# Interleaving the first two column parts at both phase changes of an encoder layer, with eight of the sixteen residual chunks turned through scratch memory

## What is computed

```
h = h + 1/2 * post1(SwiGLU_1(pre1(h)))          # 2048 -> 2*5632 -> 2048
u = pre2(h); q,k,v,gates = u @ w_in             # two kinds of attention, heads of 128
h = h + post2((sigmoid(gate_A)*A + sigmoid(gate_B)*B) @ w_out)
h = h + 1/2 * post3(SwiGLU_2(pre3(h)))
```

## Time and profile before

| | |
|---|---|
| time, median of 3 runs | 2030.08 us (2029.84 to 2030.23) |
| the profiled execution | 2030.19 us, span 2028.4 us |
| PE busy | 2019.1 us (100% of the span) |
| DVE, ACT busy | 1236.8 us (61%), 1043.1 us (51%) |
| granted TensorE clock | 0.999 |
| transfers | 445.94 MB, 220 GB/s over the span |

### The profile page before, as it was taken

How to read it: one execution, slowest core, us unless ns; L and a number is a source line. 1 busy time by engine, 2 the same in 40 slices (tenths; PEclk the granted TensorE clock), 3 DMA queues, 4 the chain that set the end, 5 groups by cost and what they waited for, 6 DMA issues and landing times.

```text
span 2028.4 us, 26583 instructions
## 1 busy us (share of the span) xinstructions
PE 2019.1 (100%) x8930; PEld 1671.7 (82%) x8930; DVE 1236.8 (61%) x1963; ACT 1043.1 (51%) x1829; POOL 49.9 (2%) x86
## 2 busy tenths in 40 slices
PE   9999999999999999999999999999999999999998
PEld 7888888888888888888888888888888888888887
DVE  6655555655555576667777676765556555555554
ACT  7445544555444564445444555665555555544443
POOL 1000000000000011110000000000000000000000
PEclk9999999999999999999999999999999999999999
DMA  8787777777556669887777777576666766675654
GB/s 303 231 232 222 214 223 221 221 228 241 196 192 193 203 201 259 257 251 214 229 231 229 224 243 232 186 230 214 216 210 214 225 222 215 216 232 195 192 193 144
DMA packets 259500, 445.94 MB, mean 220 GB/s; under 512 B 17496, under 2 KB 57688, under 8 KB 259040
## 3 DMA queue, kind: packets, MB, share of 16 engines
q1 hardware_dynamic: 254800, 432.99, 67.4%
q0 software_dynamic: 4336, 11.82, 3.0%
q10 hardware_dynamic: 288, 0.16, 0.0%
HBM read 418.42 MB, written 26.46 MB: 219 GB/s over the span
## 4 chain that ended last, share of the span: by engine, by line
PE 98%; DMA 1%; DVE 0%; ACT 0%; DVEq 0%; issue 0%; SPq 0%; ACTq 0%
PE acc L1142 32%; PE acc L1144 32%; PE acc L1143 32%; DMA raw<-in_ffn_w_in 1%; PE tp L1272 1%; PE tp L1259 1%; PE tp L1180 0%; DVE WL L761 0%; DVE h L861 0%; ACT WH L523 0%; DVE XL L767 0%; DVE fg L834 0%; DVEq L154 0%; ACT tmp L594 0%; SPq L366 0%
## 5 line engine op out<-in xcount | busy, mean ns | idle before, releaser
L761 DVE TENSOR_TENSOR WL<-raw,WH 128x512 fp32r<-128x512 f32 x1424 | 969.3, 690 | 756.0 <-ACT WH L523 754.0
L523 ACT ACTIVATE WH<-raw 128x512 fp32r<-128x512 f32 x1424 | 890.0, 631 | 935.2 <-PE acc L1144 850.6
L1142 PE MATMUL acc<-WH,XH 128*128 128x512 f32 x2030 | 794.3, 391 | 0.2
L1144 PE MATMUL acc<-WH,XL 128*128 128x512 f32 x2030 | 790.0, 389 | 0.0
L1143 PE MATMUL acc<-WL,XH 128*128 128x512 f32 x2030 | 789.9, 389 | 0.0
L1142 PEld LDWEIGHTS acc<-WH,XH 128*128 128x128 f32 x2030 | 381.2, 188 | 80.6 <-issue 1.2
L1144 PEld LDWEIGHTS acc<-WH,XL 128*128 128x128 f32 x2030 | 381.1, 188 | 79.6
L1143 PEld LDWEIGHTS acc<-WL,XH 128*128 128x128 f32 x2030 | 381.2, 188 | 78.0
L1142 PE MATMUL acc<-WH,MH 128*128 128x512 f32 x688 | 267.6, 389 | 0.0
L1143 PE MATMUL acc<-WL,MH 128*128 128x512 f32 x688 | 267.6, 389 | 0.0
L1144 PE MATMUL acc<-WH,ML 128*128 128x512 f32 x688 | 267.6, 389 | 0.0
(11 more groups left out here) (110 smaller groups left out, 649.1 us busy)
## 6 DMA issues: line engine op xcount, KB each, us to landing
raw<-in_ffn_w_in SPq DMA_DIRECT2D x350, 512.0 KB, 3.7
raw<-in_ffn_w_out SPq DMA_DIRECT2D x176, 512.0 KB, 3.6
raw<-in_w_in SPq DMA_DIRECT2D x136, 512.0 KB, 5.0
raw<-in_w_out SPq DMA_DIRECT2D x32, 512.0 KB, 4.1
turned_blocks<-Z SPq DMA_DIRECT2D x31, 512.0 KB, 3.1
Y<-turned_blocks SPq DMA_DIRECT2D x124, 128.0 KB, 4.5
raw<-in_w_up_a SPq DMA_DIRECT2D x16, 512.0 KB, 5.1
raw<-in_w_up_b SPq DMA_DIRECT2D x16, 512.0 KB, 4.2
```

The source lines that it names most:

```text
L523: act.activation(weight_hi(c), raw[:, c // 2 % RAW, c % 2, :], ACT.Copy).then_inc(hi_ready, 1)
L761: dve.tensor_tensor(weight_lo(c), raw[:, c // 2 % RAW, c % 2, :], weight_hi(c).bitcast(F32), ALU.subtract).then_inc(lo_ready, 1)
L1142: pe.matmul(a, hi[:, tok], weight_hi(c), start=first, stop=False)
L1144: return pe.matmul(a, lo[:, tok], weight_hi(c), start=False, stop=last)
```

## The change

Block b is the first column part of the new phase, block b+1 the second.

- `LATE` is 8: input chunks 8 to 15 all go through DRAM, in two halves: `Z`, `Y` for chunks 8 to 11 and `Z2`, `Y2` for 12 to 15, with a DRAM buffer and semaphores of their own. PE no longer transposes units 16 to 19.
- PE's order after the halves of c0 to c0+7 is: block b+1 with input chunks 0 to 7 (these are now c0+8 to c0+15), block b with input chunks 8 to 15 (c0+16 to c0+23), block b+1 with input chunks 8 to 15 (c0+24 to c0+31).
- DVE's two `turn_late` of `Z` stand together behind unit 15, one `split_lo` and two `turn_late` of `Z2` behind them. Both wait for the whole update of `h`. ACT's `late_hi` and DVE's `late_lo` stand behind the split of c0+20 (the first four) and of c0+22 (the other four); the sum of squares of `h` is read after the split of c0+23.
- SP stores `Z` and `Z2`, loads c0+16 to c0+19, fetches `Y`, loads c0+20 to c0+23, fetches `Y2`, and loads on.
- Blocks b and b+1 are read (`read_qkv(0)`, or `silu_gate`) after the split of c0+31; in the input projection the store and fetch of the first turned block stand behind the loads of c0+34 and c0+36. The second FFN's block b+2 stands before PE's loop, which runs one round less.

```
...
-LATE = 4
+LATE = 8
...
+    if b == B_QKV:
+        return C_QKV + DC + SKEW
...
         Y, _ = place("Y", [P, TT, NB], F32, o_yl + 8192)
+        Z2, _ = place("Z2", [P, TT, NB], F32, o_yl + 12288)
...
+            return (Y, Y2)[a // 4][:, :, :].rearrange("p t (i a s) -> p a t i s", i=4, a=4)[:, a % 4, :, :, :]
 
...
+            def enter(n, c0, weights, other, units):
+
+                load(c0, weights, 0, SKEW, 0)
+                load(c0 + SKEW, weights, 0, SKEW, other)
+                store_blocks(Z, units, 0)
+                store_second(n)
+                load(c0 + DC, weights, SKEW, 4, 0)
+                fetch_blocks(Y, units, 0)
+                load(c0 + DC + 4, weights, SKEW + 4, 4, 0)
+                fetch_second(n)
+                load(c0 + DC + SKEW, weights, SKEW, SKEW, other)
+
...
-                if not begun:
-                    load(c_in, wi, 0, DC, 0)
-                    begun = DC
+                if begun:
+                    load(c_in + begun, wi, begun - DC, 2 * DC - begun, DFF // NB)
+                else:
+                    enter(2, c_in, wi, DFF // NB, z0)
...
-                load(c_in + begun, wi, begun - DC, 2 * DC - begun, DFF // NB, 0, z0 if z0 else None, gap=0)
...
-            for b in range(QK_BLOCKS + 1):
-                if b == 1:
-                    load(C_QKV + b * DC, WIN, 0, DC, b, 0, Z_N1 + 1, gap=0)
+            enter(1, C_QKV, WIN, 1, Z_N1 + 1)
+            for b in range(2, QK_BLOCKS + 1):
+                if b == 2:
+                    load(C_QKV + b * DC, WIN, 0, DC, b, 0, Z_QK + b - 1, 0, 4, gap=2)
                 elif 2 <= b < 2 + len(QK_HEADS):
...
+                if a < 4:
+                    act.wait_ge(blocks_landed, 64 * ((Z_N1 if n == 1 else Z_N2) + 1))
+                else:
+                    act.wait_ge(second_landed, 64 * n)
...
-                for c in range(13, 15):
+                for c in range(13, DC):
                     split_hi(chunk + c)
-                for u in range(16, 20):
-                    normed_hi(n, u)
-                split_hi(chunk + 15)
                 for j in range(OUT_BLOCKS):
                     for t in range(TT):
...
-                    if j == 1:
-                        late_hi(n, 0)
-                    if j:
-                        late_hi(n, j)
+                for c in range(DC):
+                    split_hi(chunk + DC + c)
+                    if c == 4:
+                        for a in range(4):
+                            late_hi(n, a)
+                    if c == 6:
+                        for a in range(4, LATE):
+                            late_hi(n, a)
...
-                for c in range(DC):
-                    split_hi(c_in + DC + c)
-                    if n == 0 and c < 6:
-                        h_square(0, c // TT + 1, c % TT)
-                    if c == (14 if n == 0 else 8):
-                        silu_gate(b_in, norm)
+                    for c in range(DC):
+                        split_hi(c_in + DC + c)
...
+                else:
+                    silu_gate(b_in, norm, more=SKEW)
...
-            for b in range(1, QK_BLOCKS):
+            for b in range(2, QK_BLOCKS):
...
-                    if c == 5 and b >= 2:
+                    if c == (7 if b == 2 else 5):
...
-            def turn_late(n, t):
-
-                dve.wait_ge(h_ready, OUT_BLOCKS * (TT * (n - 1) + t + 1))
-                dve.transpose(Z[:, t, :].rearrange("p (j a s) -> p a j s", j=4, a=4),
-                              h[:, t, D - NB:D].rearrange("p (a j s) -> p a j s", a=4, j=4)).then_inc(blocks_turned, 1)
+            def turn_late(n, t, z, first, turned_sem):
+
+                dve.wait_ge(h_ready, OUT_BLOCKS * TT * n)
+                dve.transpose(z[:, t, :].rearrange("p (j a s) -> p a j s", j=4, a=4),
+                              h[:, t, first:first + NB].rearrange("p (a j s) -> p a j s", a=4, j=4)).then_inc(turned_sem, 1)
...
-                turn_late(n, 0)
                 scaled(b_last, n - 1, 1)
...
-                turn_late(n, 1)
...
-                for c in range(11, 14):
+                for t in range(TT):
+                    turn_late(n, t, Z, D - 2 * NB, blocks_turned)
+                split_lo(chunk + 11)
+                for t in range(TT):
+                    turn_late(n, t, Z2, D - NB, second_turned)
+                for c in range(12, DC):
                     split_lo(chunk + c)
-                for u in range(16, 20):
-                    normed_lo(n, u)
-                for c in range(14, DC):
-                    split_lo(chunk + c)
-                for a in range(LATE):
-                    late_lo(n, a)
-                dve.wait_ge(squares_ready, TT * OUT_BLOCKS * (2 * n + 1))
-                mean_square(2 * n)
+                for c in range(DC):
+                    split_lo(chunk + DC + c)
+                    if c == 4:
+                        for a in range(4):
+                            late_lo(n, a)
+                    if c == 6:
+                        for a in range(4, LATE):
+                            late_lo(n, a)
+                    if c == 7:
+                        dve.wait_ge(squares_ready, TT * OUT_BLOCKS * (2 * n + 1))
+                        mean_square(2 * n)
...
-                else:
-                    for c in range(DC):
-                        split_lo(c_in + DC + c)
...
-            for b in range(1, QK_BLOCKS):
+            read_qkv(0)
+            for b in range(2, QK_BLOCKS):
...
-                    if c == 5 and b >= 2:
+                    if c == (7 if b == 2 else 5):
...
-                    if c % 2:
-                        turn_h(n, SKEW + c + 3)
-                        turn_h(n, SKEW + c + 4)
-                for c in range(SKEW, DC):
-                    pe.wait_ge(xt_lo, units + SKEW + c + 1)
-                    chunk(c0 + c, b, XH[:, c, :], XL[:, c, :], False, c == DC - 1)
                     if c % 2 and SKEW + c + 4 < UNITS - LATE:
                         turn_h(n, SKEW + c + 3)
                         turn_h(n, SKEW + c + 4)
+                acc_free(b + 1)
+                for c in range(SKEW):
+                    chunk(c0 + SKEW + c, b + 1, XH[:, c, :], XL[:, c, :], c == 0, False)
+                for c in range(SKEW, DC):
+                    pe.wait_ge(xt_lo, units + SKEW + c + 1)
+                    chunk(c0 + SKEW + c, b, XH[:, c, :], XL[:, c, :], False, c == DC - 1)
+                for c in range(SKEW, DC):
+                    chunk(c0 + DC + c, b + 1, XH[:, c, :], XL[:, c, :], False, c == DC - 1)
 
...
-                acc_free(b_in + 1)
-                with pe.Fori(0, DFF // NB - 1) as i:
+                if n:
+                    acc_free(b_in + 1)
+                else:
+                    acc_free(b_in + 2)
+                    for c in range(DC):
+                        chunk(c_in + 2 * DC + c, b_in + 2, XH[:, c, :], XL[:, c, :], c == 0, c == DC - 1)
+                with pe.Fori(0 if n else 1, DFF // NB - 1) as i:
...
-            for j in range(1, QK_BLOCKS):
+            for j in range(2, QK_BLOCKS):
```

More of the change, by code:

```diff
@@ L217, in layer_kernel @@
         Y, _ = place("Y", [P, TT, NB], F32, o_yl + 8192)
+        Z2, _ = place("Z2", [P, TT, NB], F32, o_yl + 12288)
+        Y2, _ = place("Y2", [P, TT, NB], F32, o_yl)
         Zmix, _ = place("Zmix", [P, TT, NB], F32, o_m)
@@ L220, in layer_kernel @@
         zscr = nc.dram_tensor("turned_blocks", [TT * P * NB], F32)
+        zscr2 = nc.dram_tensor("turned_blocks2", [TT * P * NB], F32)
         rscr = nc.dram_tensor("rpb_padded", [B_H * RPB_USED * GRID_W * PADW], F32)
@@ L249, in late_turned @@
         def late_turned(a):
-            return Y[:, :, :].rearrange("p t (i a s) -> p a t i s", i=4, a=4)[:, a, :, :, :]
+            return (Y, Y2)[a // 4][:, :, :].rearrange("p t (i a s) -> p a t i s", i=4, a=4)[:, a % 4, :, :, :]
         def sem(name):
@@ L258, in layer_kernel @@
         even_landed = [sem(f"even_landed{i}") for i in range(2)]
+        second_turned, second_stored, second_landed = map(sem, ["second_turned", "second_stored", "second_landed"])
         raw_landed = [sem(f"raw_landed{i}") for i in range(RAW)]
@@ L343, in load, with store_second, fetch_second @@
                     sp.dma_start(raw[:, piece % RAW, :, :], src).then_inc(raw_landed[piece % RAW], 16)
+            def store_second(n):
+                sp.wait_ge(second_turned, TT * n)
+                sp.dma_start(zscr2[:].rearrange("(t p f) -> p t f", t=TT, p=P), Z2[:, :, :]).then_inc(second_stored, 16)
+            def fetch_second(n):
+                sp.wait_ge(second_stored, 16 * n)
+                for j in range(4):
+                    src = bass.AP(zscr2, j * P, [[NB, 32], [32 * NB, TT * 4], [1, P]])
+                    sp.dma_start(Y2[32 * j:32 * j + 32, :, :].rearrange("p t (i f) -> p (t i) f", i=4), src).then_inc(second_landed, 16)
+            def enter(n, c0, weights, other, units):
[8 more added lines that the diff above has]
```

(34 more changed lines are left out.)

## The result

The changed kernel takes 2038.39 us (median of 7 runs, 2035.92 to 2040.84) against 2030.06 (7 runs, 2029.80 to 2030.23): ratio 1.0039, 95% interval 1.0029 to 1.0049. It is slower by 8.3 us, and its times spread over 4.9 us where those of before spread over 0.4. Forecast were 2030.3 us and a range from 2027.5 to 2033.5. The profiled execution took 2038.76 us, span 2037.0. Of the runs further down, one execution of e1_late_c19 took 10083.51 us and one of e2_sp_order 5397.17; they count in the medians given there, not in the ratios.

The account below looks back on a forecast made before the run. PE bounds the kernel, busy 2019.1 of 2028.4 us. Each phase change saves 1.2 us and adds a 1.3 us wait, +0.2 us for both on the profiled execution's 2030.2, 0.1 above the median: 2030.3 us, range 2027.5 to 2033.5.

Parts of the forecast that it names:

- What the change takes off PE: At each phase change, eight transposes (0.9 us) and the wait for unit 12 (0.26 us) go: 1.2 us saved.
- the wait for unit 12: Before c0+8, PE stood 0.26 us for unit 12's remainder on DVE; moving the turn of Z removes it.
- The place and the form of the wait: At c0+16, PE waits 1.3 us for DVE's late remainder, directly behind the split of c0+20.
- c0+38: Input projection's narrow place: load behind the first turned block's fetch, costed at nothing; a rival had +1.2 us, chance 0.08.
- the peeled block: In the second FFN: no PE waits expected; the prediction falls if any appear there.
- The sum: Over both phase changes: -1.2 + 1.3 = +0.1 us at each, +0.2 us in all, 2030.3 us.
- rival (b): Transfer queue becomes the bound: c0+20 lands over 7.3 us after issue, PE waits over 3.2 us each; 2036 us, chance 0.12.
- the landing of c0+20: In SP's burst at the phase change: issued at 742.3, lands at 747.7, 5.4 us later.
- the 0.6 us until the semaphore shows a landing: At the end of c0+20's load: about 0.6 us from moved bytes at 747.1 to landing at 747.7.
- land sooner: At the second phase change: rows repeat the first 575.15 us later, except transfers, which land sooner there.
- (a): At the phase changes, c0+20 lands within 4.1 us of issue and the whole gain stays: 2027.7 us, chance 0.22.
- 2.3 us to spare: At c0+20, Y2's first late chunk is ready by 752.7, PE wants it at 755.0: no wait.

Follow-up runs that it names:

- e1_late_c19: Changed kernel with the first four late chunks split behind c0+19 instead of c0+20, on ACT and DVE: 2031.09 us, ratio 1.0002.
- e2_sp_order: Changed kernel with SP's list alone reordered: load of c0+16 ahead of the store of Z, c0+18 ahead of Z2's: 2031.31 us, ratio 1.0003.
- e1_again: The kernel of e1_late_c19 executed once more for a readable profile; that execution took 2032.22 us.
- e5: Changed kernel without the second store and fetch (Z2, Y2), the last four late chunks split from Y, so wrong columns: 2031.85 us, ratio 1.0007.
- d1_doses: Kernel before with six artificial PE waits (1 to 12 GpSimd memsets) in the second FFN's out projection: 2061.43 us, ratio 1.0153.
- e6_best: e3_both with Y2 fetched ahead of the load of c0+22 and its late chunks split behind c0+21 instead of c0+22: 2027.95 us, ratio 0.9988.
- e3_both: Changed kernel with both edits, SP's order of e2_sp_order and the first late chunks behind c0+19: 2029.37 us, ratio 0.9995.

## Why the prediction was wrong

**Right.** What the change takes off PE: 1.2 us forecast, 1.21 measured; the wait for unit 12 is gone (0.14 us between the pair at 734.43 and the next matmul, 0.39 before). There are 32 transposes instead of 48. SP's issue times were within 0.4 us (store of `Z` 737.0 and 736.99, `Z2` 738.9 and 738.77, c0+20 742.3 and 742.71). From the landing of c0+20 to PE's start on the late chunk 1.8 us were forecast and 1.8 measured (749.16 to 750.99). The place and the form of the wait were those named: c0+16, for the late remainder, directly behind the split of c0+20, which ACT had waited for. Nothing waited at the reads of blocks b and b+1, at c0+38, or in the peeled block.

**The step that failed: "The sum", which had no term for the clock.** It charged a wait its own length. The sum with the measured waits and no clock would be 2030.2 - 2.4 + 6.1 = 2033.9, inside 0.2% and 0.4 above the range; the clock's 4.7 us take it to 2038.6, where 2038.76 was measured. It was this step together with the next one: two waits of 1.3 us, as forecast, would have left the clock up, as waits of 1.02 to 1.71 us did in e1_again, e2 and e5, and the missing term would not have shown. The error is in rival (b) as well: it had the kernel more than 0.2% slower from waits of 3.2 us on, where with the clock about 2.5 us suffice. I had read the granted clock of 0.999 as a constant of the kernel, when it held only as long as PE had no such wait. d1_doses shows the term and from what length on it is there.

**The term that was mis-sized: the landing of c0+20.** 5.4 us after issue were forecast, 6.4 and 7.2 measured, and the issue itself was 0.4 us later, and so waits of 2.69 and 3.38 us instead of 1.3. I set the transfers in line at their full rate, one behind the other from 739.8. c0+16, counted to land at 743.1, landed at 744.0: the rate row has 1.1 us at half rate over the end of `Z2` and the beginning of c0+16. What slows the packets there was not tried and stays open. c0+18 landed at 745.6 (ACT's second row) instead of 744.5, and the fetch of `Y` and c0+20 took 3.5 us behind it where I had given them 3.2: `Y` moved for 2.7 us instead of 2.0, in part beside c0+20. For the 0.6 us until the semaphore shows a landing the prediction names no row; the trace has about 0.5 us (c0+20's last packet, one of 4 bytes, at 748.7, landed 749.16). That the transfers "land sooner" at the second phase change was wrong for this burst: c0+20 took 0.8 us longer there in the first profile, and in the second the longer wait was at the first phase change.

**The rivals.** (b) was the nearest, 2036 us, with a chance of 0.12; its mechanism, one store and one fetch more in the burst, holds for a part: without them (e5_no_second) the waits are about half. But the bytes do go through in time if they are ordered otherwise (e6_best), so it is a matter of order. That (b) came nearest to 2038 us is in part luck: it reached 2036 by waits of 4.1 us at the full clock, and the waits were 2.69 and 3.38. (a) did not happen in the changed kernel; its time of 2027.7 is nearly that of e6_best (2027.95), reached by another order of the lists. By the Trainium skill (DMA: Bandwidth & Descriptors, "Anatomy of one DMA") the fit that spoke for (a) is one for transfers through GpSimd; these loads are issued by SP and took 4.8 to 8.6 us against its 3.2. "2.3 us to spare" for `Y2` was wrong too, hidden by the wait ahead of it: e3_both and then e6_best laid it open.

## What to carry to other kernels

When the engine that bounds a kernel never stops, price a new wait at its length plus what the clock takes back: here under 0.2 us up to 1.7 us of waiting, and 1.5 to 3.0 us more from 2.5 us on; no wait between these two lengths was measured. So a forecast of 1.3 us with an uncertain landing behind it is not a small risk in both directions. And if data pass through a list of transfers and a list of splits, put them behind what they need and not behind what merely comes next: the data of the late chunk were there a microsecond before the weight chunk that stood in front of it, and moving it one place at both phase changes was worth 7 us.

## What the runs showed of the hardware

A wait of PE of 1.71 us or less (nine of them in the profiles, from 0.80, as the brackets count them) left the granted clock at its upper level; each of 2.53 us or more (ten) was followed by a stretch at the lower one, at 0.427 us a matmul instead of 0.227. That stretch had 6 to 14 slow matmuls (steps over 0.36 us) and did not grow with the wait: 6 behind 3.41 us, 14 behind 3.21, 12 behind 3.77, 13 behind 7.25, 10 behind 8.29. Behind the waits of 2.53 to 2.83 us the first two to six matmuls still ran at the full pace.

A 512 KB load issued around the two phase changes took 3.9 us as the first of its burst before the change, and from 4.8 to 8.6 us in the changed kernel. A load may begin to move long after its issue: c0+20 was issued at 742.71 and its first packet moved at 746.2, 3.5 us later, behind `Z2`, c0+16, c0+18 and most of `Y`.
